# PEER expert loop: the next tile's u load ahead of the v load, and layer 1's score products joined to 384 columns

## What is computed

```
def peer_ffn(tokens, wq, sub_keys, u, v):            # per chunk h of tokens
    q = (h @ wq).reshape(t, 8, 2, 128)
    s = einsum('thpd,hpnd->thpn', q, sub_keys)        # scores against 2 x 128 sub-keys
    ...                                               # top 16 of 128 x 128 experts per head: idx, gate
    act = gelu(einsum('td,thkd->thk', h, u[idx]))
    return einsum('thk,thkd->td', gate * act, v[idx])
```

## Time and profile before

| | us |
|---|---|
| median of 3 runs | 2939.14 |
| lowest and highest | 2937.1, 2950.22 |
| the profiled execution | 2943.2 |
| its span, first to last instruction | 2941.4 |

### The profile page before, as it was taken

How to read it: one execution, slowest core, us unless ns; L and a number is a source line. 1 busy time by engine, 2 the same in 40 slices (tenths; PEclk the granted TensorE clock), 3 DMA queues, 4 the chain that set the end, 5 groups by cost and what they waited for, 6 DMA issues and landing times. The chain is left out here.

```text
span 2941.4 us, 42761 instructions
## 1 busy us (share of the span) xinstructions
PE 2698.3 (92%) x14782; PEld 2307.4 (78%) x14782; DVE 2279.4 (77%) x4146; ACT 1159.3 (39%) x2016; POOL 849.8 (29%) x565
## 2 busy tenths in 40 slices
PE   7999978899788999999999999789888789999997
PEld 3888863689777899999999999664787578888886
DVE  2788877799997777778787878744898867777778
ACT  2233320433583333333333333223446445555553
POOL 0000001435453244444333333100575412212222
PEclk9999979899999999999999999899989899999999
DMA  6223225314479898888888888320356989888986
GB/s 254 106 81 128 86 87 196 119 63 158 140 218 361 325 328 316 306 308 309 305 313 309 307 305 317 143 79 6 152 172 176 380 304 323 314 314 311 321 317 221
DMA packets 247818, 682.39 MB, mean 232 GB/s; under 512 B 20172, under 2 KB 106804, under 8 KB 244020
## 3 DMA queue, kind: packets, MB, share of 16 engines
q1 hardware_dynamic: 192436, 480.00, 46.2%
q0 software_dynamic: 55296, 201.35, 19.2%
HBM read 635.34 MB, written 45.92 MB: 232 GB/s over the span
## 5 line engine op out<-in xcount | busy, mean ns | idle before, releaser
L1043 PE MATMUL bank<-h_parts,u_hi 128*128 128x384 f32 (+1 forms) x3712 | 801.0, 308 | 43.6 <-DVE u_lo L1984 31.2
L1102 PE MATMUL bank<-v_parts,p_parts 128*128 128x512 f32 x3072 | 747.0, 393 | 8.9 <-DVE p_parts L2009 8.9
L1043 PEld LDWEIGHTS bank<-h_parts,u_hi 128*128 128x128 f32 x3712 | 632.6, 192 | 73.2 <-DVE u_lo L1984 42.3
L1102 PEld LDWEIGHTS bank<-v_parts,p_parts 128*128 128x128 f32 x3072 | 580.0, 189 | 129.3 <-issue 7.3
L1043 PE MATMUL bank<-h_parts,u_lo 128*128 128x384 f32 (+1 forms) x1856 | 571.1, 308 | 0.0
L1984 DVE TENSOR_TENSOR u_lo<-arena,u_hi 128x1024 fp32r<-128x1024 f32 x208 | 254.4, 1223 | 132.3 <-ACT u_hi L1398 121.5
L1043 PEld LDWEIGHTS bank<-h_parts,u_lo 128*128 128x128 f32 x1856 | 356.7, 192 | 0.0
L2007 DVE TENSOR_TENSOR v_parts<-arena,v_parts 128x1024 fp32r<-128x1024 f32 x256 | 313.0, 1223 | 55.1 <-ACT v_parts L1488 53.3
L1398 ACT ACTIVATE u_hi<-arena 128x1024 fp32r<-128x1024 f32 x208 | 219.8, 1057 | 288.2 <-DMA arena<-in_u 288.2
L1488 ACT ACTIVATE v_parts<-arena 128x1024 fp32r<-128x1024 f32 x256 | 269.6, 1053 | 80.9 <-PE bank L1102 60.1
L2271 POOL DMA_INDIRECT arena<-in_v,arena x128 | 198.9, 1554 | 319.0 <-DVE arena L2029 295.2
(11 more groups left out here) (302 smaller groups left out, 4140.8 us busy)
## 6 DMA issues: line engine op xcount, KB each, us to landing
arena<-in_u SPq DMA_DIRECT2D x256, 512.0 KB
arena<-in_v SPq DMA_DIRECT2D x256, 512.0 KB
arena<-in_wm SPq DMA_DIRECT2D x80, 512.0 KB
arena<-in_wst SPq DMA_DIRECT2D x19, 2048.0 KB, 8.1
gate_scratch<-arena SPq DMA_DIRECT2D x18, 2048.0 KB, 8.7
arena<-gate_scratch SPq DMA_DIRECT2D x30, 768.0 KB
arena<-in_whd SPq DMA_DIRECT2D x8, 2560.0 KB, 9.1
arena<-gate_scratch SPq DMA_DIRECT2D x30, 384.0 KB
```

Of the source, the lines that this page charges most:

```text
L1043: last = mm(banks[q][:, 0:ND[p]], w[:, q, col], h[:, k, DS[p]], start=(n3 == 0), stop=(n3 == 3 * KT - 1))
L1102: last = mm(banks[2 + 2 * b + half][:, :], x[:, q, at:at + P], y[:, q, col], start=(first and i == 0), stop=(final and i == 2))
```

## The change

Two parts. **The order of loads**: `experts(j)` issues u of tile j+1 ahead of v of tile j; the first u of the loop (tile 26) is issued ahead of everything else there, in layer 1 also ahead of the layer-norm loads. The wait of each load is as before. This holds for both layers. **The form of layer 1's scores** (tiles 24 to 127 only; the early 24 keep the old form): for each k one product of the high weights with high and low tokens side by side (2 x 192 = 384 columns of the bank), and one of the low weights with the high tokens, added to the second half. The two halves of the bank are then added on VectorE, into `act_s`, and the gelu reads that. The semaphores for it are two that the recurrence of layer 0 used.

```diff
-                def experts(j, q, N):
+                def load_u(j, q, N):
                     sp.wait_ge(u_l[q], 1 + N)
                     sp.dma_start(u_raw[:, q, :], a["u"][p, j]).then_inc(u_in[q], 16)
+
+                def experts(j, q, N, more=True):
+
+                    if more:
+                        load_u(j + 1, 1 - q, N + q)
                     sp.wait_ge(v_l[q], 1 + N)
                     sp.dma_start(v_raw[:, q, :], a["v"][p, j]).then_inc(v_in[q], 16)
...
+                load_u(K0 + 2, 0, K0 // 2 + 1 + N0)
                 if p == 0:
...
-                def scores(q, N, high=u_hi, low=u_lo):
+                def scores(q, N, high=u_hi, low=u_lo, early=False):
                     pe.wait_ge(u_l[q], 1 + N + 1)
                     pe.wait_ge(s_act[q], 1 + N)
+                    if p and not early:
+                        n_t = ND[p]
+                        for k in range(KT):
+                            col = slice(k * P, (k + 1) * P)
+                            mm(banks[q][:, 0:2 * n_t].rearrange("p (x t) -> p x t", x=2), high[:, q, col], h_parts[:, :, k, DS[p]],
+                               start=(k == 0), stop=(k == KT - 1), skip_group_check=True)
+                            last = mm(banks[q][:, n_t:2 * n_t], low[:, q, col], h_hi[:, k, DS[p]], start=False, stop=(k == KT - 1),
+                                      skip_group_check=True)
+                        last.then_inc(s_pe[q], 1)
+                        return
...
-                    if own:
+                    if own and p:
+                        act.wait_ge(s_sum[q], N + (SUMMED - N0 - K0 // 2 + 1))
+                        af_(act_s[:, q, 0:ND[p]], act_s[:, q, 0:ND[p]], ACT.Gelu_apprx_tanh).then_inc(s_act[q], 1)
+                    elif own:
                         act.wait_ge(s_pe[q], N + 1)
...
+                    if own and p:
+                        dve.wait_ge(s_pe[q], N + 1)
+                        dve.wait_ge(p_do[q], 1 + N)
+                        V.tensor_reduce(act_s[:, q, 0:ND[p]], banks[q][:, 0:2 * ND[p]].rearrange("p (x t) -> p t x", x=2), AX.X, ALU.add).then_inc(s_sum[q], 1)
                     if more:
                         low_u(nq, nN)
```

More of the change, by code:

```diff
@@ L295, in build @@
         dstep = sem("vector_steps")
+        s_sum, SUMMED = [kt_pe, kt_sb], 2 * HEADS
         B_HF = 2 * WSLOT
@@ L754, in peer @@
                         mod_block(M_ALL - 4 + TAIL_M.index(j), wm_e)
-                    experts(j, j % 2, j // 2 + N0)
+                    experts(j, j % 2, j // 2 + N0, j + 1 < NK)
                 if p == 0:
@@ L1052, in peer @@
                         for q in range(2):
-                            scores(q, 2 * n + N0)
+                            scores(q, 2 * n + N0, early=True)
                         for q in range(2):
-                            scores(q, 2 * n + 1 + N0, v_hi, v_lo)
+                            scores(q, 2 * n + 1 + N0, v_hi, v_lo, early=True)
                 for n in range(nd):
```

## The result

| | before | after |
|---|---|---|
| median, us | 2940.47 (4 runs, 2937.1 to 2950.22) | **2875.02** (4 runs, 2870.32 to 2878.65) |
| ratio, 95% interval | | **0.9768** (0.9747 to 0.9790) |
| profiled execution, its span | 2943.2, 2941.4 | 2878.65, 2876.9 |
| first scores of tile 24 to first scores of tile 127, layer 1 | 545.38 | 481.95 |

The kernel is 65.5 us (2.3%) faster; 2884 was predicted, with 2862 to 2916 around it; the result lies 1 us under the narrower forecast of 2876 to 2896. A second time it took 2873.47 us, ratio 0.9771 (0.9749 to 0.9794). Of the 64.6 us between the profiled executions the loop gives 63.4.

A forecast was written before the change was run, and what follows sets the result against it. PE, busy 2698 of 2941 us, was taken to bound the kernel. Loop 490.5 instead of 545.4 (-54.9), layer 0 -1, last tile +0.5: -55.4 from the median of 2939.1, so 2884 us, range 2862 to 2916.

The forecast's parts named there:

- The price of the scores: Layer 1 scores on PE: 0.286 us a k step instead of 0.333, 0.37 less a tile, PE's floor 4.59.
- the Trainium skill's case against this part: Layer 1 scores: by N/2.4 ns + 2.5 only columns count, so joining products saves 0.02 us a tile.
- The sum on VectorE: Layer 1: one reduction of 0.555 us, taking 0.48 of DVE's time, making DVE's tile 4.45 us.
- 4.45 before any wait: DVE's layer 1 tile with the sum, in us, listed beside PE 4.59 and transfers 4.5 to 4.7.
- PE waits for u_lo behind the sum: Layer 1: sum, u_lo and signalling take 1.95 us while PE's outputs take 2.30; fits by 0.35 if DVE is free.
- u issued 2.5 us earlier: Layer 1 load queue: u goes at 2503.55 instead of 2506.07, which removes a typical ACT wait of 2.22 us.
- One transfer less stands before it: Layer 1 load queue: u, issued ahead of v, has one transfer less before it; second reason for landing earlier.
- v hardly later: Layer 1 load queue: v gets u's 512 KB before it, 2.5 us ahead, 1.3 to 1.6 us alone; hardly later.
- The entry: Start of layer 1's loop: tile 24 to 25 stays 7.6 us, 25 to 26 becomes 5.2; stall before 24 stays.
- The transfers: Layer 1 loads: 4.5 to 4.7 us a tile; 345 to 360 GB/s and ACT's u wait under 80 us expected.
- Half the stall stays, 4.73 a tile: Layer 1 loop: 0.14 us of the 0.29 stall a tile kept above PE's 4.59, for 101 tiles, 477.7 us.
- its two gains: Layer 1 loop: scores 0.37 us shorter a tile, and stall cut from 0.29 to 0.14 by earlier u, added together.

The follow-up runs named there:

- order alone: The kernel before with only the new order of loads (u of the next tile ahead of v): 2904.42 us, ratio 0.9878.
- join alone: The changed kernel with the old order of loads (u behind v), so only the joined score products and their sum: 2950.26 us, ratio 1.0029.
- after without the sum: The changed kernel with VectorE's sum left out, the gelu reading the first half of the bank: 2868.72 us, ratio 0.9748.

## Why the prediction was right, point by point

- **The price of the scores** held: a pair of 384 and 192 columns 0.285 us (0.286 said), the scores 2.25 us (2.29), PE's floor 4.55 (4.59). The sum of two widths, each from its own row, was the right way to price a shape that the trace didn't have. What the prediction called the Trainium skill's case against this part was only half of what that section says: the formula is given there as an isolated one, and weight loads are said to set the spacing too.
- **The sum on VectorE** held: 0.552 us by the mean of 97 (0.555), 0.47 in the queue (0.48). The DVE tile is 4.55 against 4.45, because v_lo starts 0.34 us after the gate product's start where it was 0.27 before, and the sum starts 0.05 us after the short instruction that ends the dot product, where u_lo started with it; together 0.1 us of a tile; and the turn of the loop (0.88 us in one tile of eight) wasn't in the sum of terms at all. With it DVE's pace is 4.66, and this is what the tile measures. "4.45 before any wait" was the one term that was too low, and DVE is not the third limit but, level with the transfers, the first.
- **"PE waits for u_lo behind the sum"**: it fits, as said (5.2 us of waits in 450).
- **u issued 2.5 us earlier** was right, and it is what breaks the chain. **"One transfer less stands before it"** was wrong as a reason where the transfer is v's: a u takes 5.5 to 5.8 us to be seen at either place. It was right where it is the gate load's (6.6 us right behind it, 5.1 and 5.3 in the tiles farthest from it), which the prediction didn't speak of.
- **v hardly later**: right; ACT never waited for v after the change.
- **The entry**: tiles 24 to 26 take 7.14 and 4.67 us where 7.61 and 7.80 stood (7.6 and 5.2 said); the stall before tile 24 stays, at 7.83.
- **The transfers** came to 359 GB/s at 0.97 (345 to 360 said), and ACT's wait for u to 47 (under 80 said).
- **Half the stall stays, 4.73 a tile**: 0.10 above PE's floor was left, not 0.14. The mis-sized terms are this one, 101 x 0.04 = 4 us, and PE's floor, 101 x 0.04 = 4 us; with the entry, 1 us shorter than said, they are the 8.5 us between 490.5 and 482.0, and nearly all of 2884 against 2875. That what was left is nearly the half that was guessed is luck: it is the turn of DVE's loop, which the prediction had no term for, and not a rest of the old stall.
- **Last tile +0.5**: +0.3 (26.2 us from the last scores to the end, 25.9 before).

What the sum didn't see, though its total came out, is that **its two gains weren't separate**. It counted 37 us for shorter scores, 15 for half of the stalls and 3 at the entry. Measured in the loop: order alone -31, join alone +15, both -63. So the join is worth -32 on top of the order and less than nothing without it. The prediction's own rows had the chain: in the earlier trace rows each u goes out about 1 us behind a v (2500.01 and 2500.98, 2504.93 and 2506.07), that v had waited for v_lo, and ACT waited for the u. It read those rows as "u comes late", a loss to be halved, and not as a loop whose length sets the pace. The total didn't suffer because the change cuts the chain and shortens the scores at once, and that is luck. Had the change been the join alone, the same sum would have said about 2900 and been wrong by 50 us.

## What to carry to other kernels

When an engine's wait for a load is long although no engine and no queue is full, follow the load back to what let it be issued: if that ends in the same load's consumer two slots ago, the length of that circle, divided by its tiles, can be the pace, and work taken off the bound engine then brings nothing until it is cut. Look at the tiles one by one too: a loss that sits in every fourth points at what only every fourth has. Price two parts of a change together and each alone, and ask for each whether it pays only where the other is in. When the next limits lie within 3% (here DVE 4.66, transfers, PE 4.55), taking one away shows nothing; take away two at once to see the third.

## What the hardware did that wasn't expected

**Beside narrow products the granted clock stayed low.** In the kernel with 128-column scores PE was busy without a gap for 123 us ahead of the loop (2128.7 to 2251.6), at a granted clock of 0.50 (1.2 GHz); with the same code and 192 columns (order alone) it was idle in between, and the granted clock was 0.86 to 0.93. The stretches by PE alone (length, busy time with instructions, granted clock, DMA share, GB/s), first with 128 columns, then with 192:

```profile
2130.00:2180.00 50.00, 50.00 (x237) 0.50 0.41 133
2180.00:2230.00 50.00, 50.00 (x236) 0.50 0.39 124
```
```profile
2130.00:2180.00 50.00, 39.57 (x310) 0.86 0.51 162
2180.00:2230.00 50.00, 44.37 (x363) 0.93 0.49 152
```

237 products in 50 us are 0.21 us each, twice the 0.110 of the loop. The first joint scores came at 2406.8 instead of 2362.8 us: 44 of the 50 us between the two profiled executions (the loop gives the other 6). An engine that is always busy doesn't get the full clock by that alone. Why it stayed low with these products wasn't tried further.

**A load of 512 KB takes 5 to 7 us from issue to use**, by the medians, in this loop, and the share of the transfers doesn't tell which. Where ACT was waiting, the median for u was 5.50 us before (share 0.89) and 5.77 after (0.97), but 6.99 with the order alone (0.93, 68 tiles) and 6.57 after without the sum (0.96, 75 tiles). Why these two are longer wasn't tried.

**A short GpSimd instruction lengthens VectorE's.** One of 1.04 us per tile made the two-input VectorE instruction on a gathered row 0.35 to 0.41 us longer (1217 and 1278 to 1625 ns).
